# No side steps at the end of the forget gate's groups and at the start of a branch projection, and later splits of branch B's gated tiles

## What is computed

```python
(q_a, k_a, v_a, z_a, q_i, k_i, w_i, q_b, f_b, i_b, z_b, gates) = split(rms_norm(x) @ w_in)
o_a = dsa_attention(...)            # indexer scores, top-k choice of keys, softmax, weighted sum
y_a = o_a * silu(z_a)
f   = lb + (1 - lb) * sigmoid(f_b)  # the forget gate of branch B
o_b = hgrn2_chunkwise(silu(q_b), 1 - f, i_b, log(f))   # a gated recurrence
y_b = rms_norm(o_b) * silu(z_b)
merged = sigmoid(g_a) * (y_a @ w_branch_a) + sigmoid(g_b) * (y_b @ w_branch_b)
out = x + merged @ w_out
```

## Time and profile before

| | us |
|---|---|
| median of 3 runs (1906.74 to 1909.43) | 1908.15 |
| the profiled execution | 1908.92 |
| its span, first to last instruction | 1907.6 |
| TensorE busy | 1890.0 (99%) |
| VectorE busy | 1174.7 (62%) |
| ScalarE busy | 880.1 (46%) |
| GpSimd busy | 323.6 (17%) |

### The profile page before, as it was taken

How to read it: one execution, slowest core, us unless ns; L and a number is a source line. 1 busy time by engine, 2 the same in 40 slices (tenths; PEclk the granted TensorE clock), 3 DMA queues, 4 the chain that set the end, 5 groups by cost and what they waited for, 6 DMA issues and landing times.

```text
span 1907.6 us, 37116 instructions
## 1 busy us (share of the span) xinstructions
PE 1890.0 (99%) x15758; PEld 1857.5 (97%) x15758; DVE 1174.7 (62%) x1709; ACT 880.1 (46%) x1265; POOL 323.6 (17%) x317
## 2 busy tenths in 40 slices
PE   9999999999999999999999999999999999999999
PEld 8999999999999999999999999999999999999987
DVE  7765665656554556755654766676467776655744
ACT  6544454544444444544454543446443333444543
POOL 3220110202110003400221243040011132110300
PEclk9999999999999999999999999999999999999999
DMA  7566555566666666666565565563564444666664
GB/s 262 165 211 182 158 154 165 167 188 191 197 191 195 198 190 188 194 204 193 196 232 195 177 217 168 149 178 119 156 187 140 138 141 142 183 199 195 193 232 154
DMA packets 180752, 347.31 MB, mean 182 GB/s; under 512 B 11742, under 2 KB 24410, under 8 KB 180058
## 3 DMA queue, kind: packets, MB, share of 16 engines
q1 hardware_dynamic: 178938, 340.67, 58.8%
q10 hardware_dynamic: 1648, 4.26, 0.6%
HBM read 334.89 MB, written 6.29 MB: 179 GB/s over the span
## 4 chain that ended last, share of the span: by engine, by line
PE 92%; DVE 3%; SPq 1%; issue 1%; DMA 1%; ACT 1%; POOL 1%; POOLq 0%; ACTq 0%; DVEq 0%
PE bank L1326 91%; DVE w_lo L1973 1%; SPq L1300 1%; DMA scratch<-arena 1%; DMA w_raw<-in_w_in 1%; ACT w_hi L1665 1%; DVE hb L2215 0%; SPq L1259 0%; POOL stats L2533 0%; DVE arena L2079 0%; DVE scratch L2079 0%; ACT L1733 0%; POOL scratch L2583 0%; PE bank L1547 0%; ACT ob L1825 0%
## 5 line engine op out<-in xcount | busy, mean ns | idle before, releaser
L1973 DVE TENSOR_TENSOR w_lo<-w_raw,w_hi 128x1024 fp32r<-128x1024 f32 (+2 forms) x644 | 792.8, 1235 | 460.5 <-ACT w_hi L1665 458.6
L1665 ACT ACTIVATE w_hi<-w_raw 128x1024 fp32r<-128x1024 f32 (+2 forms) x644 | 662.8, 1032 | 854.5 <-PE bank L1326 839.7
L1326 PE MATMUL bank<-hb,w_hi 128*128 128x256 f32 x5284 | 954.5, 278 | 1.7 <-DVE hb L1997 1.6
L1326 PEld LDWEIGHTS bank<-hb,w_hi 128*128 128x128 f32 x5284 | 813.8, 188 | 3.7 <-DVE w_lo L1973 2.2
L1326 PE MATMUL bank<-ob,w_hi 128*128 128x256 f32 (+1 forms) x4060 | 767.7, 283 | 5.0 <-DVE ob L2269 1.7
L1326 PE MATMUL bank<-hb,w_lo 128*128 128x256 f32 x2448 | 677.5, 277 | 0.0
L1326 PEld LDWEIGHTS bank<-ob,w_hi 128*128 128x128 f32 x4060 | 633.2, 188 | 9.1 <-DVE w_lo L1973 2.3
L1326 PE MATMUL bank<-ob,w_lo 128*128 128x256 f32 (+1 forms) x2224 | 621.6, 279 | 0.0
L1326 PEld LDWEIGHTS bank<-hb,w_lo 128*128 128x128 f32 x2448 | 460.9, 188 | 0.0
L1326 PEld LDWEIGHTS bank<-ob,w_lo 128*128 128x128 f32 x2224 | 418.4, 188 | 0.0
L1326 PE MATMUL bank<-w_hi,ob 128*128 128x512 f32 (+1 forms) x384 | 104.4, 359 | 1.0 <-DVE arena L2079 1.0
(11 more groups left out here) (241 smaller groups left out, 1019.6 us busy)
## 6 DMA issues: line engine op xcount, KB each, us to landing
w_raw<-in_w_in SPq DMA_DIRECT2D x436, 512.0 KB, 3.8
w_raw<-in_w_out SPq DMA_DIRECT2D x64, 512.0 KB, 4.2
w_raw<-in_w_o_conv SPq DMA_DIRECT2D x32, 512.0 KB, 4.0
w_raw<-in_w_o_mla SPq DMA_DIRECT2D x32, 512.0 KB, 4.0
w_raw<-in_w_branch SPq DMA_DIRECT2D x32, 512.0 KB, 4.4
w_raw<-in_w_kv_b SPq DMA_DIRECT2D x16, 512.0 KB, 4.6
w_raw<-in_w_q_b SPq DMA_DIRECT2D x16, 384.0 KB, 3.5
arena<-x_kept SPq DMA_DIRECT2D x2, 2048.0 KB, 9.0
```

What stands on the lines that cost most here:

```text
L1326: return nc.tensor.matmul(dst, lhsT, rhs, start=start, stop=stop, skip_group_check=True)
L1665: act(dst, src, ACT.Copy).then_inc(S_("w_hi"), 1)
L1973: tt(low, src, high.bitcast(F32), ALU.subtract).then_inc(S_("w_lo"), 1)
```

## The change

- `Phase` has a new number `calm`. In `run`, a pump is left out after a group's last unit where `calm` is negative, and after a phase's first `calm` units where it is positive. fb has -1 (two pumps less), ba has 3 (three less). The jobs lose no stage; all later stages come at later pumps.
- The splits of "yb" come 9 tiles after the gate instead of 7; "zm" keeps 9, "ya" 7.
- The scratch ring has 6 buffers instead of 5. `ob` is 8992 instead of 9216 elements long for each partition; nothing beyond its new end was used.

```diff
--- before.py
+++ after.py
@@ -189,9 +189,10 @@
 class Phase:
 
 
-    def __init__(self, name, weight, groups, ktiles, operand, n, period=1, pairs=False, hold=False):
+    def __init__(self, name, weight, groups, ktiles, operand, n, period=1, pairs=False, hold=False, calm=0):
         self.name, self.weight, self.groups, self.ktiles = name, weight, groups, ktiles
         self.operand, self.n, self.period, self.pairs, self.hold = operand, n, period, pairs, hold
+        self.calm = calm
 
 
 class Unit:
@@ -240,12 +241,12 @@
     put("ka", "w_in_2", groups_of(C2_KA, 1), KT, "h2_all", T)
     put("va", "w_in_2", groups_of(C2_VA, 1), KT, "h2_all", T)
     put("qa2", "w_in_2", groups_of(C2_QA, 2), KT, "h2", S)
-    put("fb", "w_in_2", groups_of(C2_FB, 2), KT, "h2_all", T)
+    put("fb", "w_in_2", groups_of(C2_FB, 2), KT, "h2_all", T, calm=-1)
     put("ib", "w_in_2", groups_of(C2_IB, 2), KT, "h2_all", T)
     put("qb", "w_in_2", groups_of(C2_QB, 2), KT, "h2", S)
     put("ga", "w_in_2", groups_of(C2_G, 4), KT, "h2", S)
     put("za", "w_in_2", groups_of(C2_ZA, 2), KT, "h2", S)
-    put("ba", "w_branch_a", groups_of(0, 4), 8, "ya", S)
+    put("ba", "w_branch_a", groups_of(0, 4), 8, "ya", S, calm=3)
     put("zb", "w_in_2", groups_of(C2_ZB, 2), KT, "h2", S)
     put("gb", "w_in_2", groups_of(C2_G + D, 4), KT, "h2", S)
     put("bb", "w_branch_b", groups_of(0, 4), 8, "yb", S)
@@ -269,7 +270,7 @@
     add, done = plan.add, plan.done
     ph = phases()
     units = plan.units = units_of(ph)
-    banks, side, scratch, heads = Ring(5), Ring(3), Ring(5), Ring(3)
+    banks, side, scratch, heads = Ring(5), Ring(3), Ring(6), Ring(3)
     stats, prob, prob_t, prob_m = Ring(6), Ring(2), Ring(2), Ring(2)
     issued, lows = {"load": 0, "split": 0}, deque()
     pending, active, deferred = deque(), [], deque()
@@ -350,7 +351,8 @@
                     out[m].ends(evac(u.g, m, out[m].slot, s["proj"]))
             if not (p.hold and i == p.end - 1):
                 split_to(i + N_SPLIT)
-            if (i - p.first) % p.period == p.period - 1:
+            at_end, at_start = p.calm < 0 and u.last, i - p.first < p.calm
+            if (i - p.first) % p.period == p.period - 1 and not at_end and not at_start:
                 pump()
 
 
@@ -676,7 +678,7 @@
                 later(gate_y, wait)
             else:
                 gate_y()
-            later(split_y, 9 if name == "zm" else 7)
+            later(split_y, 7 if name == "ya" else 9)
             return s["evac"]
         return evac
 
@@ -1082,7 +1084,7 @@
         hb_all = sb("hb", [P, ODD + 2 * KT * S + ODD], F32R)
         hb = hb_all[:, ODD:ODD + 2 * KT * S].rearrange("p (k n) -> p k n", k=2 * KT)
         self.hb_hi, self.hb_lo = hb[:, 0:KT, :], hb[:, KT:2 * KT, :]
-        ob_all = sb("ob", [P, 2 * KT * (T + ODD)], F32R)
+        ob_all = sb("ob", [P, H2_AT + (KT + H2_LOW) * H2_STEP], F32R)
         ob = ob_all[:, H2_AT + NMETA:H2_AT + NMETA + 2 * KT * S].rearrange("p (k n) -> p k n", k=2 * KT)
         self.ob_hi, self.ob_lo = ob[:, 0:KT, :], ob[:, KT:2 * KT, :]
         mg2 = ob_all[:, MG2_AT:MG2_AT + 2 * KT * S].rearrange("p (k n) -> p k n", k=2 * KT)
@@ -1097,7 +1099,7 @@
         self.rope1 = sb("rope1", [P, 2, S])
         self.fac = sb("factor", [P, 3, T])
         self.small = sb("small", [P, 256])
-        self.scratch = [sb(f"scratch{i}", [P, T])[:, :] for i in range(5)]
+        self.scratch = [sb(f"scratch{i}", [P, T])[:, :] for i in range(6)]
         self.heads = [sb(f"head_factor{i}", [P, T])[:, :] for i in range(3)]
         self.acc_a, self.acc_b = sb("acc_a", [P, S])[:, :], sb("acc_b", [P, S])[:, :]
         psum = [ctx.enter_context(nc.psum_tensor(f"bank{i}", [P, 512], F32))[:, :] for i in range(8)]
```

## The result

The changed kernel took **1916.47 us** (median of four runs, 1914.25 to 1918.10) beside 1908.19 for the kernel before, a ratio of 1.0047 (95% interval 1.0035 to 1.0058): 8.3 us slower, where 3.5 us of gain were forecast and the range ended at 1907.3. The profiled execution took 1914.25 us with a span of 1912.9.

A forecast was written before the change was run, and what follows sets the result against it. TensorE, busy 99% of the span, was taken as the bound, so only its waits could be won back. Gains of 1.95 + 0.1 + 1.40 = 3.45 us gave 1904.7 us from 1908.15; the 8-in-10 range was 1902.6 to 1907.3.

The forecast's parts named there:

- Part 1: Forget gate fb, two pumps left out: two TensorE waits of 0.30 and 1.65 us go, gain 1.95 us.
- attention's wait returns: Rival: softmax, mix and turn meet ib's evacuations, one wait of 1.65 us comes back; 1906.4 us, chance 0.19.
- Part 2: Branch A's projection ba, three pumps left out: waits of 2.69 us become one of 2.60, gain 0.1 us.
- the risk below zero: In ba, a loss from leaving out three pumps; the forecast gave none, its gain bounded by 0 and 2.7 us.
- The bound of 0 from below: Lowest gain forecast for ba's three omitted pumps: 0, with ya 5 still late; the upper bound was 2.7 us.
- Part 3: Branch B's later yb splits: two TensorE waits of 0.70 us, in zb and gb, go entirely; gain 1.40 us.
- Part 4: Sixth scratch buffer, buffers behind ob moved: no wait seen ended by a scratch being freed, so gain 0.
- a rival at 0.07: Slow TensorE pace in qb and from ba's last units to bb's end: 8.4 us more, 1913.1 us, chance 0.07.
- if long stretches step at 0.118: Sign of a wrong forecast: long TensorE stretches stepping at 0.118 us a matmul that had stepped at 0.113.
- The sum: Whole kernel: gains 1.95 + 0.1 + 1.40 = 3.45 us, giving 1904.7 us.
- gb keeps the fast pace for its whole length now: In gb, the forecast's argument against the slow-pace rival, whose chance was 0.07.

The follow-up runs named there:

- e2: The kernel before with only fb's two pumps left out, the sixth scratch buffer and the shorter ob: 1911.46 us, ratio 1.0010.
- e3: The kernel before with only ba's first three pumps left out, five scratch buffers kept: 1911.27 us, ratio 1.0019.
- before: The kernel without the change, against which each timed kernel ran: 1908.19 us beside the changed kernel.
- e4: The kernel before with only the splits of yb moved to 9 tiles, five scratch buffers kept: 1905.59 us, ratio 0.9992.
- after: The changed kernel with all of the change, against the kernel before: 1916.47 us, ratio 1.0047; measured again later 1915.31 us, ratio 1.0030.
- e1: The kernel before with only the sixth scratch buffer and the shorter ob, every engine's order unaltered: 1911.77 us, ratio 1.0023.
- e5: The whole change with the sixth scratch buffer allocated directly behind ob, against the kernel before: 1914.47 us, ratio 1.0027.
- e7: The kernel before with only ob 896 bytes shorter, five scratch buffers kept: 1907.91 us, ratio 0.9998.
- e14: The whole change with the sixth scratch buffer allocated last, against the kernel before: 1908.23 us, ratio 1.0006.
- e16: The kernel before with fb's and yb's edits, sixth scratch directly behind ob, one added broadcast matmul after cin0's last unit: 1911.15 us, ratio 1.0019.
- e13: The changed kernel plus two broadcast matmuls after qb's second unit and one after zb's second: 1907.07 us, ratio 0.9994 to the kernel before.

## Why the prediction was wrong, step by step

- **Part 1: right.** Forecast 1.95 us; fb and ib together took 2.13 less, in e2 too. One table load instead of three stands on ScalarE between 1280 and 1300 us (the earlier trace rows show two of the three, the first was at 1288.28):

```profile
1291.73 0.43 ACT L1897 ACTIVATE arena<-scratch 128x272 f32<-128x272 f32 x1 [0.25 <-DVE scratch L2081]
1292.06 2.00 ACT L1667 ACTIVATE w_hi<-w_raw 128x1024 fp32r<-128x1024 f32 x2
1294.08 1.28 ACT L1735 ACT_TABLE_LOAD   x1
```

The "attention's wait returns" rival did not come: no gap like those of the earlier trace rows.
- **Part 2: mechanism right, no gain.** The three waits of the earlier trace rows became one ahead of ba's third unit, ended by VectorE's low halves behind rec_scale and a w_lo, as read from the earlier trace rows:

```profile
1587.79 0.28 PE L1328 MATMUL bank<-hb,w_lo 128*128 128x256 f32 x1
1590.77 0.48 PE L1328 MATMUL bank<-hb,w_hi 128*128 128x256 f32 x2 [2.71 <-DVE hb L2217]
```
```profile
1586.28 0.95 DVE L2398 TENSOR_TENSOR arena<-arena 128x256 f32<-128x256 f32 x1 [2.15 <-POOL arena L2625]
1587.26 0.84 DVE L2400 TENSOR_TENSOR arena<-arena 128x256 f32<-128x256 f32 x1
1588.03 1.74 DVE L1975 TENSOR_TENSOR w_lo<-w_raw,w_hi 128x1024 fp32r<-128x1024 f32 x1
1589.69 1.61 DVE L2217 TENSOR_TENSOR hb<-arena,hb 128x256 fp32r<-128x256 f32 x3
```

Its size is 2.98 less 0.12, 2.86 us, against 2.60 forecast and 2.69 removed. The stage says that it came out even: ba took 53.32 us, less 0.6 for its slow units 52.7, as before. The mis-sized term is the risk below zero. In ba the granted clock fell behind the one long wait in four of nine profiles and behind two waits of 1.2 to 1.4 us in none of eleven; where it fell, part 2 loses 1.3 to 1.6 us (e3, part 2 alone: ba is 2.1 us longer than in before, 0.6 of it slow pace). The bound of 0 from below was too kind.
- **Part 3: right.** No wait is left in zb and gb; alone (e4) both stages took 1.41 us less together (0.71 and 0.70), 1.40 forecast. In after one low half stands ahead of the w_lo that the earlier trace rows had behind three, and this w_lo ended at 1665.50; TensorE began the unit that uses it at 1666.58. The three halves behind it took 0.54 us each instead of the 0.41 forecast, and no wait came of it:

```profile
1662.86 0.96 DVE L2217 TENSOR_TENSOR hb<-arena,hb 128x256 fp32r<-128x256 f32 x1
1663.74 1.76 DVE L1975 TENSOR_TENSOR w_lo<-w_raw,w_hi 128x1024 fp32r<-128x1024 f32 x1
1665.42 1.62 DVE L2217 TENSOR_TENSOR hb<-arena,hb 128x256 fp32r<-128x256 f32 x3
```

- **Part 4 and the pace: the step that failed.** The prediction put part 4 at 0 ("no row prices an address") and named its nearest row, the two paces of the earlier trace rows, as a rival at 0.07. The rival's mechanism and size were right, 8.4 us against 9.0, and its sign of being wrong ("if long stretches step at 0.118") is what the trace shows. The term of 0 measured 4 us by itself (e1), and 9.0 in after, where part 3 has taken away the wait that ended the slow pace in e1. The chance of 0.07 was too small. The sum took the pace of each stretch as a property of its stage, though the earlier trace rows showed two for the same matmul. Its argument "gb keeps the fast pace for its whole length now" says only that a pace lasts; it holds for the slow one as well. What the runs showed instead: a long quiet stretch keeps the pace that the last side step before it left, and an edit that moves a buffer or a step can change which one that is. Part 3 took away the waits that can end a slow stretch and so made the stake larger: from ba's eleventh unit to the end of bb 70 units times 0.107 = 7.5 us, and qb's 1.6 beside it. Of the ten kernels other than before that have no added step in these stages (after, e1 to e5, e7, e14 to e16), four entered zb slow and five ran qb slow. Looking back, a chance near a half would have been nearer than 0.07, and before was one of the kernels in which both had fallen well. What in the buffers' places or in the ring of six sets the pace stays open.

A page of the Trainium skill bears on the distance. "TensorE: Matmul & The Clock Gate", section "Back-to-back issue gap", has columns over 2.4 GHz plus about 2.5 ns for a matmul by itself, an estimated 109 ns for 256 columns; for a stream of weight loads and matmuls it has about 81 ns at 128 columns and about 131 at 512. These traces have 113.3 and 117.8 ns for 256 columns at a granted clock of 1.00. Both lie above the first figure and between the other two, and they are two paces for the same matmul where the section gives one.

## What to carry to other kernels

Where the busiest engine has no waits left, look at its rate (instructions in a quiet stretch of fixed length) before you look at its waits: a change of a few tenths of a per cent can be all rate, and moving a buffer that nobody waits for can cost more than the waits that the edit removes. Such a version should be tried in two or three placements of its buffers before the idea in it is judged; here the same four parts gave 1915, 1914 or 1908 us by where the sixth buffer lay. And gathering several short waits of TensorE into one long one gained nothing here and brought a fall of the granted clock in four of nine profiles.

## What was unexpected of the hardware

- TensorE has two steady distances between like matmuls at one granted clock of 1.00, 113.3 and 117.8 ns (2.72 and 2.83 us for 24). The fast one was held for up to 590 us, the slow one for 200. They switch at side steps and at waits, but not at each, and in no profile inside the quiet stretches of qb, zb, gb and bb or in the 590 us. One added matmul of 128 x 128 (two in the profile), with no wait, turned 38 us of zb, and gb's 87 and bb's 44 stayed turned behind it (e13). Why, no run here tells: by place of buffers, by added steps and by moved steps it can be changed, and none of these alone foretells it.
- After one idle of 2.86 us in ba the granted clock fell to 0.50 for about 3 us in four of nine profiles; two waits of 1.2 to 1.4 us, some 5 us apart, did it there in none of eleven. Elsewhere a shorter one was enough at times: the clock fell behind a distance of 1.23 us between two matmuls at 1153 us (e5) and of 1.27 at 1149 (e7), where other profiles passed one of 1.2 to 1.4 without a fall.
